# Norm factors made on a 128x8 column tile and spread by TensorE, and one FFN weight tile split before the first gating

## The reference

```
def rmsnorm(x, g):
    xf = x.astype(jnp.float32)
    y = xf * lax.rsqrt(jnp.mean(xf * xf, axis=-1, keepdims=True) + EPS)
    return (y * g.astype(jnp.float32)).astype(x.dtype)

def layernorm(x, g, b, eps=1e-5):
    xf = x.astype(jnp.float32)
    mu = jnp.mean(xf, axis=-1, keepdims=True)
    xc = xf - mu
    var = jnp.mean(xc * xc, axis=-1, keepdims=True)
    y = xc * lax.rsqrt(var + eps) * g.astype(jnp.float32) + b.astype(jnp.float32)
    return y.astype(x.dtype)

def swiglu(h, w_gate, w_up, w_down):
    return (jax.nn.silu(h @ w_gate) * (h @ w_up)) @ w_down
...
    h = rmsnorm(x, g_pre) * (1.0 + scale[:, None]) + shift[:, None]      # norm 0
    ...
    x = x + gate[:, None] * rmsnorm(y, g_post)                           # norm 1
    for layer in range(DEPTH_2):
        h = rmsnorm_2(x, mix_norm[layer])                                # norms 2 and 4
        ... attention and pooling mixer, or conformer_conv with layernorm (norm 5)
        h = rmsnorm_2(x, ffn_norm[layer])                                # norms 3 and 6
        x = x + swiglu(h, ffn_w_gate[layer], ffn_w_up[layer], ffn_w_down[layer])
    return rmsnorm_2(x, final_norm)                                      # norm 7
```

## Time and profile before

| | us |
|---|---|
| median of 3 runs | 3724.18 (3724.14 to 3729.88) |
| the profiled execution: its time | 3728.57 |
| the profiled execution: its span | 3726.9 |
| TensorE busy in the span | 3345.0 (90%) |
| VectorE busy | 1567.6 (42%) |
| ScalarE busy | 677.8 (18%) |
| mean granted TensorE clock | 0.91 |

### The profile page before, as it was taken

How to read it: one execution, slowest core, us unless ns; L and a number is a source line. 1 busy time by engine, 2 the same in 40 slices (tenths; PEclk the granted TensorE clock), 3 DMA queues, 4 the chain that set the end, 5 groups by cost and what they waited for, 6 DMA issues and landing times. The chain is left out here.

```text
span 3726.9 us, 36700 instructions
## 1 busy us (share of the span) xinstructions
PE 3345.0 (90%) x15223; PEld 2433.5 (65%) x15223; DVE 1567.6 (42%) x2254; ACT 677.8 (18%) x1123; POOL 80.4 (2%) x148
## 2 busy tenths in 40 slices
PE   2999999787779989979799999997996799999996
PEld 2444564363345578867688888886854678888885
DVE  5002462133331165562544343448974543434435
ACT  1102350121111145551100000012124200000002
POOL 0000010000010030000000000000000000000000
PEclk6997589978878989979899999998998899999998
DMA  6001000000121000011111111101100111111111
GB/s 218 28 28 35 1 1 17 15 12 12 34 68 45 22 1 1 1 59 49 45 46 56 45 45 56 45 23 40 40 14 29 51 46 57 45 45 45 56 34 45
DMA packets 128899, 144.79 MB, mean 39 GB/s; under 512 B 18535, under 2 KB 118795, under 8 KB 127499
## 3 DMA queue, kind: packets, MB, share of 16 engines
q1 hardware_dynamic: 128491, 134.72, 11.5%
q10 hardware_dynamic: 288, 8.39, 0.5%
HBM read 134.71 MB, written 8.39 MB: 38 GB/s over the span
## 5 line engine op out<-in xcount | busy, mean ns | idle before, releaser
L1022 PE MATMUL ps<-h_high,w_high 128*128 128x512 f32 x1408 | 551.6, 392 | 44.5 <-DVE h_low L1973 30.3
L1022 PE MATMUL ps<-h_high,w_low 128*128 128x512 f32 x1408 | 550.6, 391 | 0.0
L1022 PE MATMUL ps<-h_low,w_high 128*128 128x512 f32 x1408 | 550.5, 391 | 0.0
L646 PE MATMUL ps<-ht,ring 128*128 128x512 f32 (+1 forms) x1056 | 465.8, 602 | 22.1 <-ACT ht L1187 9.8
L646 PEld LDWEIGHTS ps<-ht,ring 128*128 128x128 f32 (+1 forms) x1056 | 195.7, 187 | 288.7 <-issue 280.6
L999 PE MATMUL ps<-h_high,ring_parts 128*128 128x512 f32 x1024 | 321.6, 396 | 52.3 <-DVEq L363 30.2
L1022 PEld LDWEIGHTS ps<-h_high,w_high 128*128 128x128 f32 x1408 | 266.4, 189 | 103.7 <-issue 48.3
L1022 PEld LDWEIGHTS ps<-h_high,w_low 128*128 128x128 f32 x1408 | 266.4, 189 | 55.3
L1022 PEld LDWEIGHTS ps<-h_low,w_high 128*128 128x128 f32 x1408 | 266.1, 189 | 55.6
L1022 PE MATMUL ps<-act_high,w_high 128*128 128x512 f32 x704 | 273.9, 389 | 0.0
L1022 PE MATMUL ps<-act_high,w_low 128*128 128x512 f32 x704 | 273.9, 389 | 0.0
(11 more groups left out here) (296 smaller groups left out, 3923.0 us busy)
## 6 DMA issues: line engine op xcount, KB each, us to landing
ring<-in_ffn_w_gate_dram SPq DMA_DIRECT2D x22, 1024.0 KB, 5.3
ring<-in_ffn_w_up_dram SPq DMA_DIRECT2D x22, 1024.0 KB, 5.3
ring<-in_ffn_w_down_dram SPq DMA_DIRECT2D x22, 1024.0 KB, 4.9
ring<-in_w_mod_dram SPq DMA_DIRECT2D x8, 1536.0 KB, 6.3
ring<-in_conv_w_pw_dram SPq DMA_DIRECT2D x24, 512.0 KB, 4.0
ring<-in_w_in_dram SPq DMA_DIRECT2D x3, 1536.0 KB, 7.8
big<-in_x_dram SPq DMA_DIRECT2D x2, 2048.0 KB, 10.5
ring<-in_w_in_dram SPq DMA_DIRECT2D x4, 1024.0 KB, 6.4
```

Source lines behind the costliest of these rows:

```text
L646: last = mm(o[0:m, 512 * half:512 * half + 512], w(k), src(k)[:, 512 * half:512 * half + 512], start=k == 0, stop=k == kk - 1)
L1022: return mm(o, w, rows, start=start and part_ == 0, stop=stop and part_ == 2)
```

## The change

For every norm, the sum of squares is turned by TensorE: each 128x128 block of the sum row is the stationary operand and one column of ones the moving one, so that eight matmuls with one output column each leave the 1024 token sums as a tile of 128 tokens x 8 columns. ScalarE's root and VectorE's reciprocal then work on 128x8 elements. `spread` brings the factors back to all partitions in the order of a row: for each of 8 blocks, the column of factors, broadcast along the free dimension to 128x128, is the stationary operand, and the identity matrix is the moving one; the result goes to PSUM banks 6 and 7. VectorE's multiplications read the factors from there and no longer from `sc[:, 3]`.

In `sum_square` the copy for k = 0 is gone; the add for k = 1 takes both squares. The layer norm uses the same path: VectorE subtracts the mean straight from PSUM with one `scalar_tensor_tensor`, ScalarE's copy of the mean is gone, VectorE adds the squares, and TensorE's 16 matmuls of L1131 are replaced by `norm_sum`. In the FFN, tile 2 is split between tile 1 and `hidden(0)`, behind a wait for group 0's gates.

```
+        root_sum, root_col = misc[:, 272:280], misc[:, 280:288]
...
+            def spread(n):
+
+                pe.wait_ge(s.rs_made, n + 1)
+                for t in range(TB):
+                    last = mm(ps[:, 3072 + P * t:3072 + P * t + P], root_col[:, t:t + 1].to_broadcast([P, P]), ident[:, :],
+                              start=True, stop=True)
+                last.then_inc(s.rs_wide, 1)
+
             def norm_sum(n):
 
                 pe.wait_ge(s.sq_used, 8 * n + 8)
-                for half in range(2):
-                    last = mm(bank(6 + half), ones[:, :], sc[:, 2, 512 * half:512 * half + 512], start=True, stop=True)
+                for t in range(TB):
+                    last = mm(ps[:, 3072 + t:3073 + t], sc[:, 2, P * t:P * t + P], ones[:, 0:1], start=True, stop=True)
                 last.then_inc(s.sum_done, 1)
+                if n:
+                    spread(n)
 
             norm_sum(0)
 
@@ -679,6 +691,7 @@
             for n in range(24):
                 last = mm(ps[:, 512 + n:513 + n], mod_sum[:, P * n:P * n + P], ones[:, 0:1], start=True, stop=True)
             last.then_inc(s.mod_done, 1)
+            spread(0)
...
             stage(pe, "convolved")
-            for k in range(KC):
-                pe.wait_ge(s.sq_ready, 8 * 5 + k + 1)
-                for half in range(2):
-                    last = mm(bank(6 + half), ones[:, :], sc[:, k % 2, 512 * half:512 * half + 512],
-                              start=k == 0, stop=k == KC - 1)
-                last.then_inc(s.sq_used, 1)
+            norm_sum(5)
...
             def root(n, eps=EPS):
 
-                if n == 5:
-                    a.wait_ge(s.sq_used, 8 * n + 8)
-                else:
-                    a.wait_ge(s.sum_done, n + 1 - (n > 5))
-                f(sc[:, 3, :], bank(6, 2), ACT.Sqrt, bias=eps, scale=1.0 / D).then_inc(s.rs_ready, 1)
+                a.wait_ge(s.sum_done, n + 1)
+                f(root_sum, ps[:, 3072:3072 + TB], ACT.Sqrt, bias=eps, scale=1.0 / D).then_inc(s.rs_ready, 1)
...
-            a.wait_ge(s.mean_done, 1)
-            f(sc[:, 2, :], bank(2, 2), ACT.Copy, scale=1.0 / D).then_inc(s.mean_copied, 1)
...
             def sum_square(n, k):
 
+                if k == 0:
+                    return
                 v.wait_ge(s.sq_ready, 8 * n + k + 1)
-                if k == 0:
-                    v.tensor_copy(sc[:, 2, :], sc[:, 0, :]).then_inc(s.sq_used, 1)
+                if k == 1:
+                    tt(sc[:, 2, :], sc[:, 0, :], sc[:, 1, :], add).then_inc(s.sq_used, 2)
...
             def root(n):
 
                 v.wait_ge(s.rs_ready, n + 1)
-                chain(v.reciprocal(sc[:, 3, :], sc[:, 3, :]))
+                v.reciprocal(root_col, root_sum).then_inc(s.rs_made, 1)
+                v.wait_ge(s.rs_wide, n + 1)
 
             def scaled(src, g0, dst, gains=cols, made=s.h_ok):
                 for k in range(KC):
-                    stt(dst[:, k, :], src[:, k, :], gains[:, g0 + k:g0 + k + 1], sc[:, 3, :], mul, mul).then_inc(made, 1)
+                    stt(dst[:, k, :], src[:, k, :], gains[:, g0 + k:g0 + k + 1], bank(6, 2), mul, mul).then_inc(made, 1)
...
             def middle(l, i, group_, add_before=True):
 
                 q = 3 * group_ - 1
-                split_tile(l, i, q)
                 if add_before:
+                    split_tile(l, i, q)
                     for k in range(KC):
                         add_down(l, i, group_ - 2, k)
...
                 split_tile(l, 0, 0)
                 normed(norm, gain)
                 split_tile(l, 0, 1)
+                v.wait_ge(s.gate_out, N_F[l] + 2)
+                split_tile(l, 0, 2)
                 hidden(l, 0, 0)
                 middle(l, 0, 1, add_before=False)
...
-            v.wait_ge(s.mean_copied, 1)
             planes = lambda row: row.rearrange("p (two m) -> p two m", two=2)
-            for k in range(KC):
-                tt(zc[:, k], zc[:, k], planes(sc[:, 2, :]), sub).then_inc(s.xc_done, 1)
+            added_and_squared(5, lambda k: stt(zc[:, k], planes(bank(2, 2)), -1.0 / D, zc[:, k], mul, add)
+                              .then_inc(s.xc_done, 1))
             low(T_PW2)
             low(T_PW2 + 1)
             root(5)
```

More of the change, by code:

```diff
@@ L212, in build @@
         s.rs_ready = sem("rs_ready")
+        s.rs_made = sem("rs_made")
+        s.rs_wide = sem("rs_wide")
         s.sum_done = sem("sum_done")
@@ L297, in build @@
         s.mean_done = sem("mean_done")
-        s.mean_copied = sem("mean_copied")
         s.xc_done = sem("xc_done")
@@ L1762, in first_added @@
             def first_added(k):
-                chain(stt(ht[:, k, :], ht[:, k, :], misc[:, 48 + k:49 + k], sc[:, 3, :], mul, mul))
+                chain(stt(ht[:, k, :], ht[:, k, :], misc[:, 48 + k:49 + k], bank(6, 2), mul, mul))
                 tt(xt[:, k, :], xt[:, k, :], ht[:, k, :], add).then_inc(s.x_add, 1)
@@ L1968, in normed @@
                             v.wait_ge(s.h_ok, H_OK[norm] + k - 1)
-                        stt(sc[:, k % 2, :], xt[:, k, :], cols[:, gain + k:gain + k + 1], sc[:, 3, :], mul, mul)\
+                        stt(sc[:, k % 2, :], xt[:, k, :], cols[:, gain + k:gain + k + 1], bank(6, 2), mul, mul)\
                             .then_inc(s.h_mul, 1)
@@ L2078, in _ @@
                 if k < KC:
-                    tt(zc[:, k], zc[:, k], planes(sc[:, 3, :]), mul).then_inc(s.h_mul, 1)
+                    tt(zc[:, k], zc[:, k], planes(bank(6, 2)), mul).then_inc(s.h_mul, 1)
                 if k >= 1:
```

## The result

The changed kernel takes **3678.84 us** (median of 4 runs, 3678.49 to 3681.6). The kernel before took 3727.03 us on the same chip (3724.14 to 3732.21). The ratio is 0.9871, with a 95% interval of 0.9854 to 0.9888: 48 us less, 42 to 54. 41.2 us less and a time of 3683.0 were predicted.

What follows compares the result with a forecast made beforehand. TensorE was busy 3345.0 of 3726.9 us, so gains had to lie in its standstills (at most 382 us) or half-clock stretches. Terms: 18.5 + 18.0 + 2.2 + 1.1 + 1.4 = 41.2 us off 3724.18, giving 3683; whole range 3669 to 3700.

Steps and rivals of the forecast that it cites:

- The tile split, 18.5 us: In the FFNs, splitting tile 2 earlier removes two TensorE waits, 14.3 us, and keeps its clock, 4.2 us.
- A norm, 3.0 us: Norms 1, 2, 3, 4, 6 and 7: 7.59 us of root and reciprocal out, 0.23 + 0.20 + 4.1 + 0.05 in.
- `spread` at half clock: In the norms, spread's 16 records were priced at half clock, 4.1 us, rather than 2.3 at full clock.
- the rival: In the norms, spread runs at full clock because its dense work raises the clock: 3669 to 3676 us, chance 0.14.
- The bound at full clock: Best case in the norms: spread at full clock gains 8 times 1.8 us more, 3668.6 us.
- No extra time for the broadcast column: In spread, records with a broadcast column were taken to overlap; over 0.35 us apart would make the prediction wrong.
- The 9.2 us bound: Worst case for spread: 16 records that don't overlap, up to 0.578 us each; 41 us worse, 3724.
- the rivals built on it (3703, 3753): Spread slow in part, about 6.7 us: 3703, chance 0.08; its weight load and multiplication one after the other: 3753, chance 0.03.
- The one-column sum, 3.6 to 3.7: In the norms, eight one-column matmuls (16 records) take 3.6 to 3.7 us, as the two wide ones did (3.69); nothing gained.
- The factor from PSUM, no cost: In the norms, VectorE's multiplications read the factor from PSUM without loss: 1.280 us against 1.285 with no PSUM source.
- The copy, 1.1 us: Dropping the 0.60 us copy for k = 0 gains 1.1 us, in line only in norms 2 and 0.
- The layer norm, 1.4 us: The layer norm's new path brings its first multiplication from 2816.77 to 2815.3, 1.4 us gained.

Runs made afterwards that it cites:

- experiment 1: The kernel before with only the third tile's split moved ahead of the first gating, old norms kept: 3705.96 us against 3725.95.
- experiment 2: The changed kernel with the third tile's split put back behind the first gating, so the norms' change alone: 3697.83 us, 28.1 less than before.
- experiment 3: The kernel before with the reciprocal on 8 columns instead of 1024, written to scratch, so the norms aren't computed: 3675.38 us, 50.6 less.
- Experiment 4: The changed kernel with every spread made twice, 32 records where there were 16: 3699.14 us, 20 more than the changed kernel.
- experiment 5: The changed kernel with four dense filler matmuls on TensorE ahead of the sum (three in the layer norm, none in norm 0): 3671.8 us.
- experiment 8: The changed kernel with the layer norm's mean, sum, root and reciprocal as in the kernel before, other norms as changed: 3680.4 us.

## Why the prediction was right, point by point

- **Place and mechanism.** The time lay in TensorE's standstills at the norms and in two stalls of the FFNs. Experiments 1, 2 and 3 show both parts alone: 20.0 us, 28.1 us, and 50.6 for the bare reciprocal.
- **The tile split, 18.5 us.** Right to 0.3 us. Between the gate copies the traces have 8.8 and 9.9 us less, 18.7 together. The stalls are 14.3 of it; the clock kept gives the rest, 4.4 where 4.2 was said. The other 1.0 us that the table has for the first FFN was not the split's. In the runs experiment 1 has 20.0, with 16 to 26 as its interval.
- **A norm, 3.0 us.** 3.6 in the mean of the six. For norm 7: from the start of the root to the multiplication 7.75 us before, 4.40 now, where 7.59 and 4.58 were put. `spread` had been priced at 4.1 by L805's eight records doubled, and took 3.78. The records follow each other at 0.213 us in both, and what the first and the last of a row take beyond that, 0.36 us together, comes once for 16 and not twice. The handovers of the old chain were worth 0.16 more than its bare durations, and those of the new one 0.24 where 0.05 was put. The sum became 0.11 shorter here, where nothing was put, and more where the clock fell only after its start (3.05 in norm 3).
- **`spread` at half clock.** Right in the changed kernel. Experiment 4 shows how near the rival was: 16 records more, and the clock rises within them. The bound at full clock was put at 1.8 us less; experiment 5's 2.05 us confirms it (1.73).
- **No extra time for the broadcast column.** The records overlap as those of L805 do, 0.213 us apart, where over 0.35 would have made the prediction wrong. The 9.2 us bound and the rivals built on it (3703, 3753) were wrong.
- **The one-column sum, 3.6 to 3.7.** 3.57 at half clock, and 1.95 in experiment 5 once TensorE was kept at work. By the Trainium skill (TensorE: Matmul & The Clock Gate, section LDWEIGHTS) a load of 128 columns is 107 ns, and 16 of them an estimate of 1.7 us. That is near the time at full clock, and the forecast was right to go by the rows at half clock for this kernel.
- **The factor from PSUM, no cost.** 1.275 us for the earlier trace rows's 1.280 and 1.285. The layer norm's subtraction from PSUM took 1.218 and its multiplication 1.216 as well. With its operand in SBUF each of these two took 1.220 before. The Trainium skill (VectorE: DVE Perf Modes, section The TRN2 errata) gives a PSUM source 62 cycles more, an estimate of 0.065 us; the traces don't agree with it for these float32 instructions.
- **The copy, 1.1 us.** Half of it was wrong: 0.65 in norm 2, while in norm 0 nothing shows, since the modulation's last sum came no earlier (86.92 us, 83.93 before) and sets what follows.
- **The layer norm, 1.4 us.** 2.2 in the traces, and 1.2 to 1.6 in the runs of experiment 8. The eight subtractions and seven adds took 17.6 us where 17.9 was put, the sum 3.54 and the spread 3.78 where 3.7 and 4.1 were.
- **Not foreseen:** 1.7 us in the output. ScalarE's copies there waited 7.7 us in all for the transfers of the output before, and 4.4 now. Kernels with the old norms had 31 to 32 us for this tail, the others 29 to 30; why wasn't tested.

The measured 3678.8 is 4.2 us below the forecast. The gain of 48.2 us was forecast 7.0 too small, just below its interval of 42 to 54. In the traces the terms were together 5.6 us too small, of which 3.6 are the six norms' and 1.0 was chance in the first FFN; the output added 1.7. That the time still came out within 4.2 us is in part luck: the forecast started from a median of 3724.18, and the median of the kernel before over all four runs is 3727.03.

## What to carry to other kernels

An elementwise result that is the same in all 128 partitions should be made once, on the smallest tile, when the engine pays by the element: here 6.55 us became 0.20. Then price what brings it back to full width, for that is the new link: of the 7.59 us taken out, half went to `spread` (3.78 us), and one function on the wide row was better still (1.02). Where TensorE stands idle for a few us ahead of a short link that it does itself, dense filler work can nearly halve that link (the sum 3.57 to 1.95 us), provided the filler ends before the link's own data is there. The sums of all seven filled norms became that short, but only in two of them did `spread` behind the sum follow.

## What the runs showed of the hardware

- VectorE's reciprocal costs 6.25 ns an element in a row: 0.202 us for 8, 0.35 for 32, 6.55 for 1024. ScalarE's root takes 0.178 us for 8 columns and 1.02 for 1024.
- A matmul with a broadcast column as its stationary operand overlaps with its neighbours as the other ones of 128 columns (L805) do: 16 records in 3.78 us at half clock, in 2.05 at full.
- One-column matmuls follow the clock in the same ratio (3.57 and 1.95 us for 16). Shortening the 0.5 us behind them to 0.18 did not bring the spreads to full clock.
- The same code took 709.5 and 717.1 us in the attention part in two executions, and 710.5 and 714.7 in two others. With profiles of one execution each, a difference of that size in a part that wasn't touched says nothing.
